# Head outputs turned in an earlier step of the head loop, and half of the first output-projection products put among the samples' small products

## The reference, cut to what matters

```python
for l in range(DEPTH):                                  # 2 layers
    hn = rmsnorm(xp, norm_mix[l])
    q_nope, q_rope, c_kv, k_r, qb, kb, vb, g = project_in(hn, pos_p, w_in[l], ...)
    a_out = mla_prompt(q_nope, q_rope, c_kv, k_r, w_ukv[l])                 # 6 heads x 64
    b_out = combine_dilations([dilated_prompt(qb, kb, vb, w, d) ...])       # 6 heads x 64
    c_out = conv_module(g_ext, conv_w[l], conv_b[l], conv_ln_g[l], ...)     # 256 channels, layer norm, silu
    xp = xp + jnp.concatenate([a_out, b_out, c_out], axis=-1) @ w_out[l]    # (256 x 1024) @ (1024 x 1024)
    hf = rmsnorm(xp, norm_ffn[l])
    xp = xp + peer_blocked(hf, peer_wq[l], peer_subkeys[l], peer_u[l], peer_v[l])
    ...                                                 # the 8 sample tokens likewise, against cache and windows
```

## Time and profile before

| | |
|---|---|
| median of 3 runs | 2055.27 us (2052.07 to 2057.17) |
| profiled execution: its time / its span | 2057.03 us / 2055.2 us |
| mean granted TensorE clock in it | 0.993 of full speed |
| PE busy | 2035.2 us (99%) |
| PEld busy | 1806.4 us (88%) |
| DVE busy | 1551.5 us (75%) |
| ACT busy | 1291.0 us (63%) |
| POOL busy | 121.5 us (6%) |

### The profile page before, as it was taken

How to read it: one execution, slowest core, us unless ns; L and a number is a source line. 1 busy time by engine, 2 the same in 40 slices (tenths; PEclk the granted TensorE clock), 3 DMA queues, 4 the chain that set the end, 5 groups by cost and what they waited for, 6 DMA issues and landing times.

```text
span 2055.2 us, 40772 instructions
## 1 busy us (share of the span) xinstructions
PE 2035.2 (99%) x15562; PEld 1806.4 (88%) x15562; DVE 1551.5 (75%) x3543; ACT 1291.0 (63%) x2567; POOL 121.5 (6%) x140
## 2 busy tenths in 40 slices
PE   9999999999999999999999999999999999999998
PEld 7777899999999888788887779999999998887887
DVE  6855789868899776676678466989588996766766
ACT  5456345658888666565564554565688876655654
POOL 2200010000000010100022000000000001101000
PEclk9999999999999999999999999999999999999999
DMA  9354357776666898898764633677767668988886
GB/s 329 142 172 154 135 170 255 244 250 222 218 208 219 290 313 289 295 322 281 250 229 143 204 133 124 214 255 251 245 215 219 216 214 307 314 284 295 268 270 219
DMA packets 137376, 481.76 MB, mean 234 GB/s; under 512 B 25666, under 2 KB 42082, under 8 KB 130768
## 3 DMA queue, kind: packets, MB, share of 16 engines
q1 hardware_dynamic: 124640, 438.45, 63.8%
q0 software_dynamic: 10496, 40.42, 5.6%
q10 hardware_dynamic: 2048, 0.30, 0.1%
HBM read 475.83 MB, written 104.21 MB: 282 GB/s over the span
## 4 chain that ended last, share of the span: by engine, by line
PE 97%; DVE 1%; ACT 1%; issue 0%; DMA 0%; ACTq 0%; DVEq 0%
PE ps L1235 36%; PE ps L1282 33%; PE ps L849 4%; PE ps L937 3%; PE ps L1247 3%; PE ps L1198 2%; PE ps L945 2%; PE ps L1206 2%; PE ps L1202 2%; PE ps L1162 1%; PE ps L893 1%; PE ps L1036 1%; PE ps L1221 1%; PE ps L902 1%; ACT region L1463 1%; PE ps L996 1%
## 5 line engine op out<-in xcount | busy, mean ns | idle before, releaser
L2231 DVE TENSOR_TENSOR parts<-region,parts 128x1024 fp32r<-128x1024 f32 x512 | 625.7, 1222 | 300.5 <-ACT parts L1559 298.6
L1235 PE MATMUL ps<-tokens_hi,parts 128*128 128x256 f32 x4096 | 760.5, 284 | 0.0
L1559 ACT CAST parts<-region 128x1024 fp32r<-128x1024 f32 x512 | 538.8, 1052 | 270.9 <-PE ps L1282 198.3
L1282 PE MATMUL ps<-parts,parts_hw 128*128 128x512 f32 x3024 | 688.7, 389 | 0.0
L1282 PEld LDWEIGHTS ps<-parts,parts_hw 128*128 128x128 f32 x3024 | 566.7, 188 | 124.1 <-DVE parts_hw L2281 6.9
L1235 PEld LDWEIGHTS ps<-tokens_hi,parts 128*128 128x128 f32 x4096 | 636.6, 188 | 1.0 <-issue 0.5
L1235 PE MATMUL ps<-parts_hw,parts 128*128 128x256 f32 x2048 | 573.7, 280 | 0.0
L1235 PEld LDWEIGHTS ps<-parts_hw,parts 128*128 128x128 f32 x2048 | 386.5, 189 | 0.0
L1605 ACT ACTIVATE big<-ps 128x256 f32<-128x256 f32 (+31 forms) x252 | 131.7, 523 | 146.9 <-PE ps L1235 146.9
L1593 ACT CAST parts_hw<-big 128x256 fp32r<-128x256 f32 x256 | 171.0, 668 | 0.7 <-DVE big L2292 0.7
L1586 ACT ACTIVATE region<-region 128x128 f16<-128x128 f16 x512 | 169.2, 436 | 0.0
(11 more groups left out here) (329 smaller groups left out, 2228.8 us busy)
## 6 DMA issues: line engine op xcount, KB each, us to landing
region<-in_peer_uT SPq DMA_DIRECT2D x256, 512.0 KB, 4.0
region<-in_peer_v SPq DMA_DIRECT2D x256, 512.0 KB, 4.8
out<-in_state_win_k SPq DMA_DIRECT2D x112, 384.0 KB, 5.0
out<-in_state_win_v SPq DMA_DIRECT2D x112, 384.0 KB, 5.0
big<-in_window_keysT SPq DMA_DIRECT2D x16, 576.0 KB, 5.6
big<-in_state_win_v SPq DMA_DIRECT2D x48, 192.0 KB, 4.0
region<-in_w_out SPq DMA_DIRECT2D x4, 2048.0 KB, 7.8
big<-in_peer_wq SPq DMA_DIRECT2D x4, 2048.0 KB, 11.2
```

The costliest lines, as they stand in the source:

```text
L1235: mm = pe.matmul(ps[:, j % ZB, 0:SEQ], a, hp[b][:, c, :], start=(c == 0 and n == 0), stop=(c == KD - 1 and n == 2))
L1282: mm = pe.matmul(ps[:, 2 * half + t, :], w_t[a][:, 128 * t:128 * t + 128], v_t[b][:, 512 * half:512 * half + 512], start=(j == 0 and n == ...
L1559: act.copy(hi_t[n % HIGHS], rows_t[n % ROWS]).then_inc(high[l], 1)
L2231: dve.tensor_tensor(lo_t[n % ROWS], rows_t[n % ROWS], hi_t[n % HIGHS], ALU.subtract).then_inc(low[l], 1)
```

## The change

Four of the six `mT` jobs move from behind the loop into step 11, ahead of `ow`; the fifth goes to step 12; the sixth stays behind the loop. The products of `out_high(0, 0)` for k = 0 to 3 move into step 12, ahead of `owT`, and those of `out_high(0, 1)` for k = 0 to 3 into step 13, ahead of `olT` (eight products each). ACT's eight weight casts and four of its casts of head outputs move into step 11, ahead of its reads of `ow`; DVE's low parts move likewise. The banks from the last `PT` to the output projection are dealt out over six banks, so that the two of the projection's first sums stay free. One block of weights (k = 5) gets another place in memory.

```diff
+EARLY = 4
...
         if s == WINDOW_MIX:
+            jobs += [(("mT", g), "V") for g in range(EARLY)]
             jobs += [(("ow", 0), "A"), (("ow", 1), "A")]
         if s == WINDOW_MIX + 1:
             jobs += [(("owT",), "V"), (("wT",), "V")]
+            jobs += [(("mT", EARLY), "V")]
...
-    jobs += [(("mT", g), "V") for g in range(2 * HP)]
+    jobs += [(("mT", EARLY + 1), "V")]
...
+    if NUM["PT", 2 * NH - 1] <= n < NUM["xo", 0, 0]:
+        return BESIDE_OUT[(n - NUM["PT", 2 * NH - 1]) % 6]
...
                     if s == WINDOW_MIX:
+                        wait_moved(pe, "O", 2 * EARLY - 1)
+                        for g in range(EARLY):
+                            turn_heads(g)
                         mix_window(0)
                         mix_window(1)
                     if s == WINDOW_MIX + 1:
+                        wait_moved(pe, "mT", EARLY - 1)
+                        out_high(0, 0, 0, EARLY)
                         wait_moved(pe, "ow", 1)
...
+                        wait_moved(pe, "O", 2 * EARLY + 1)
+                        turn_heads(EARLY)
                     if s == WINDOW_MIX + 2:
+                        out_high(0, 1, 0, EARLY)
                         pe.wait_ge(wsel_ready, 1)
...
                 wait_moved(pe, "O", 2 * NH - 1)
-                for g in range(2 * HP):
-                    turn("mT", g, parts=[...])
+                turn_heads(EARLY + 1)
...
                 for t in range(2):
-                    out_high(0, t)
+                    out_high(0, t, EARLY, KD)
...
                     if s == WINDOW_MIX:
+                        for g in range(EARLY):
+                            high_heads(g)
+                        act.wait_ge(product[now[0]], NUM["S", 2 * NH - 1] + 1)
+                        out_weights_high(0)
                         for n, dst in enumerate((owS, owS2)):
...
+                    if s == WINDOW_MIX + 1:
+                        high_heads(EARLY)
...
-                out_weights_high(0)
-                for g in range(2 * HP):
-                    ...
+                high_heads(EARLY + 1)
```

More of the change, by code:

```diff
@@ L155, with bank_of @@
 LATE = {("z", 0, 0): 0, ("z", 0, 1): 1, ("z", 0, 2): 2, ("z", 1, 2): 3, ("s", 0, 3): 4, ("s", 1, 3): 5, ("slot", 0): 6, ("pT",): 7, ("pr",): 6, ("slot", 1): 7, ("hB", 0): 4, ("hB", 1): 5, ("gy",): 6}
-BANK = [LATE.get(name, (n if n < NUM["mT", 0] else n + 6) % 8) for n, (name, _) in enumerate(JOBS)]
+OUT_BANK = [(NUM["xo", 0, t] + 6) % 8 for t in range(2)]
+BESIDE_OUT = [b for b in range(8) if b not in OUT_BANK]
+def bank_of(n, name):
+    if name in LATE:
+        return LATE[name]
+    if NUM["PT", 2 * NH - 1] <= n < NUM["xo", 0, 0]:
+        return BESIDE_OUT[(n - NUM["PT", 2 * NH - 1]) % 6]
+    return (n if n < NUM["os",] else n + 6) % 8
+BANK = [bank_of(n, name) for n, (name, _) in enumerate(JOBS)]
 PRIOR = [max([m for m in range(n) if BANK[m] == BANK[n]], default=None) for n in range(len(JOBS))]
@@ L364, in out_high_part @@
                 return rounded[24576][:, 512 * k:512 * k + 512]
-            return rounded[4096][:, 4096 + 512 * k:4608 + 512 * k] if k < 6 else rounded[11392][:, 512 * k - 3072:512 * k - 2560]
+            return rounded[4096][:, 4096 + 512 * k:4608 + 512 * k] if k < 5 else rounded[11392][:, 512 * k - 2560:512 * k - 2048]
         def out_low_part(c, k):
@@ L1085, in mix_window, with turn_heads, out_high @@
                               skip_group_check=True).then_inc(product[now[0]], 1)
+                def turn_heads(g):
+                    turn("mT", g, parts=[(oAB[:, t, 128 * g:128 * g + 128], 128, 128, 128 * t) for t in range(2)])
+                def out_high(c, t, k0, k1):
+                    o = begin("xo", c, t) if k0 == 0 else bank("xo", c, t)
+                    for k in range(k0, k1):
+                        pe.wait_ge(wo_high, KD * c + k + 1)
+                        if c == 0 and k == 2 * HP:
+                            wait_moved(pe, "ycT", 1)
+                        for i, part in enumerate((hiT, mix_lo)):
+                            pe.matmul(o[:, 0:512], part[:, k, 128 * t:128 * t + 128], out_high_part(c, k), start=(k == 0 and i == 0), stop=False,
+                                      skip_group_check=True)
                 for s in range(2 * NH + 2):
@@ L1139, in _ @@
                 wait_moved(pe, "O", 2 * NH - 1)
-                for g in range(2 * HP):
-                    turn("mT", g, parts=[(oAB[:, t, 128 * g:128 * g + 128], 128, 128, 128 * t) for t in range(2)])
+                turn_heads(EARLY + 1)
                 wait_moved(pe, "olT")
@@ L1154, in _ @@
                 wait_moved(pe, "os")
[L1155 to L1163, removed]
                 def out_low(c, t):
@@ L1454, in _, with out_weights_high, high_heads @@
                     act.copy(va[:, t, :], o[:, 0:384]).then_inc(moved_a[now[0]], 1)
+                def out_weights_high(c):
+                    act.wait_ge(w_ld[now[0]][(5 + c) % 2], 16 * ((5 + c) // 2))
+                    for k in range(KD):
+                        act.copy(out_high_part(c, k), wview(5 + c)[:, k, :]).then_inc(wo_high, 1)
+                def high_heads(g):
+                    o = arrive(act, "mT", g)
+                    act.copy(hiT[:, g, 0:SEQ], o[:, 0:SEQ]).then_inc(mix_high, 1)
                 for s in range(2 * NH + 2):
@@ L1514, in _ @@
                             act.copy(yt[0:m, t, :], o[0:m, 0:CC]).then_inc(moved_a[now[0]], 1)
+                    if s == WINDOW_MIX + 1:
+                        high_heads(EARLY)
                     if s == CONV_STEP[3]:
                         roots(5, slice(9, 12))
[L1517 to L1520, removed]
-                out_weights_high(0)
-                for g in range(2 * HP):
-                    o = arrive(act, "mT", g)
-                    act.copy(hiT[:, g, 0:SEQ], o[:, 0:SEQ]).then_inc(mix_high, 1)
+                high_heads(EARLY + 1)
                 for c in range(2):
@@ L1992, in conv_out, with low_heads @@
                         wait_moved(dve, "ycT", c)
+                def low_heads(g):
+                    o = read("mT", g)
+                    dve.wait_ge(mix_high, g + 1)
+                    dve.tensor_tensor(mix_lo[:, g, 0:SEQ], o[:, 0:SEQ], hiT[:, g, 0:SEQ], ALU.subtract).then_inc(moved_v[now[0]], 1)
                 for s in range(2 * NH + 2):
@@ L2023, in _ @@
                         part_logits()
+                    if s == WINDOW_MIX:
+                        for g in range(EARLY):
+                            low_heads(g)
                     if s == WINDOW_MIX + 1:
@@ L2026, in _ @@
                         part_weights()
+                        low_heads(EARLY)
                     if s == WINDOW_MIX + 2:
@@ L2035, in _ @@
                         conv_norm()
[L2036 to L2039, removed]
+                low_heads(EARLY + 1)
                 o = read("os")
```

2 lines of the change are left out of this document (1 added, 1 removed).

## The result

The changed kernel takes 2058.80 us (median of 9 runs, 2057.43 to 2062.33), the kernel before 2052.15 beside it (9 runs, 2051.61 to 2057.17): a ratio of 1.0029, with a 95% interval of 1.0020 to 1.0037, or 6.0 us more. That is no difference by the bound of 0.3% set ahead, though only just, and all of the interval lies on the slow side. The forecast was 2058.0, made as 2.8 us on a median of 2055.27: the time is met, the difference is twice as large.

What follows compares the result with a forecast made beforehand. PE carries 97% of the chain, then hands over to DVE in the output projection. That hand-over 1.4 us later in each of two layers gives +2.8 us on the median of 2055.27: 2058.0 us, range 2052 to 2063.

Steps and rivals of the forecast that it cites:

- The mechanism: Output projection: PE waits for `conv_out` with 12 high products queued behind, the first nine at 1.2 GHz; 1.4 us later per layer.
- The hand-over to DVE: Layer 0's output projection: DVE carries the chain from 197.88 us, so its earlier or later start shifts all behind.
- Three signs of being right: PE idle 2 to 4 us for `conv_out`; `conv_out` ending some 2.6 us later; second `add_out` 0.1 to 2.0 later.
- the cost of a layer: Up to DVE's hand-over: 1.4 us later per layer, bounds 0.1 if the clock holds, 2.0 if all 12 run at 1.2.
- In the kernel before this hides: Convolution's chain before the change: PE needs it only with its 13th product, near 189.3 us, after `conv_out` ends at 188.24.
- the path to the last `mT` product: Steps 11 to 13 on PE: last `mT` product near 184.7 us against 182.1, 2.6 us later.
- What stands behind the start of the batch: From `conv_out`'s end at 190.8: 12 high products to 195.3, then 16 low products and the pipeline, 3.9 us, to 199.2.
- all products behind the new wait begin at 1.2 GHz: Products behind PE's wait for `conv_out`: the skill's rule that each burst after a wait begins cold; gives the 1.4 us.
- The clock holds: Rival: wide products among small ones keep 2.4 GHz, back at once after the wait; +0.1 us a layer, 2055.5 us; chance 0.29.
- No wait: Rival: PE's wait for the convolution doesn't bind, low clock's price returns; 4.3 us earlier a layer, 2046.7 us; chance 0.05.
- Early fall: Rival: clock falls near 182 us, in the second early batch; 4.5 taken, 2064.3 us; chance 0.14.

Runs made afterwards that it cites:

- convolution early: Changed kernel with the convolution's norm, transposes, sigmoid, `conv_out` and last head pair ahead of the second eight early products, `os` behind the high products: 2047.02 us, ratio to before 0.9971.
- the version with the convolution's products last: Changed kernel with the first tile's products for k = 6 and 7 behind the second tile's k = 4 and 5: 2055.60 us, ratio to before 1.0013.
- its longer chain: Kernel before with `conv_out`'s first DVE instruction of the first 128 tokens run three times instead of once: 2055.92 us, ratio to before 1.0019.
- the heads alone early: Changed kernel with the sixteen early output-projection products put back behind the convolution's transposes: 2054.13 us, ratio to before 1.0007.
- the convolution early with the products late: Version with the convolution's part moved ahead, but its sixteen early products put back behind the convolution's transposes: 2053.22 us, ratio to before 0.9998.

## Why the prediction was right, and where its sizes were off

The stage by execution, us after the exponential of head 11 (PE's start behind its wait for the convolution, the wait in brackets, and DVE's second `add_out`):

| execution | layer 0 | layer 1 |
|---|---|---|
| before, first | no wait, 30.89 | no wait, 30.89 |
| before, second | 21.23 (1.69), 29.88 | 21.01 (1.47), 29.70 |
| before, third | no wait, 30.93 | 20.19 (1.74), 28.84 |
| after, first | 24.50 (1.80), 33.00 | 24.40 (2.07), 33.32 |
| after, second | 24.39 (3.48), 32.55 | 24.39 (1.80), 33.12 |
| convolution early | no wait, 27.40 | no wait, 27.39 |

The means are 30.19 before and 33.00 after: 2.8 us in a layer, 5.6 in both, of the 6.0 measured (4.1 to 7.6 by the interval).

**Right.** The mechanism is the one that was forecast. The hand-over to DVE does set the layer: from layer 0's second `add_out` to layer 1's exponential all executions without a fall of the clock in between agree within 0.5 us (986.6 to 987.04). PE waits for the last instruction of `conv_out` in both layers, 1.8 and 2.1 us, with 12 high products behind it, 1.2 GHz in the wait, and the first of these products 0.43 apart, eight and a half and ten and a half of the twelve (nine forecast). The clock stood at 1.00 from 175 to 181.9. ACT's copy of head 10's probabilities held PE for 0.62 us ahead of the fourth early pair (0.6 forecast), and the last page did not wait for `ow` 0: no idle time stands ahead of its row at 172.60. The weights landed in time as in the earlier trace rows (median 7.8 us after their issue), and ACT's casts of the query weights, 1.5 us later in the stage than before (188.12), were done long before DVE came to them (197.76). Three signs of being right were met in kind but not in size: the waits of 1.80 and 2.07 us lie at or under the lower end of 2 to 4, `conv_out` ended 3.1 and 2.6 us later against some 2.6, and the second `add_out` came 2.1 and 2.4 us later against 0.1 to 2.0.

**The term that was mis-sized: the cost of a layer, forecast 1.4 us, measured 2.8 (2.1 and 2.4 between the two first traces).** The sum had a layer end 32.2 us after the exponential (199.2 less 166.99), against 30.89 before. The means are 33.00 and 30.19. So some 0.7 us is missing on either side.

The first is "In the kernel before this hides". The earlier trace rows bear that out, but for that execution alone, whose clock was low for 10 us in both layers. In three layers of six PE waits for the convolution in the kernel before as well. The stage I started from was one of the long ones: 30.89 against 30.19 in the mean.

The second is the path to the last `mT` product and on to the last batch. By the prediction's times `conv_out` ends at 190.8, 23.8 us after the exponential; the batch began 24.39 to 24.50 after it in all four layers. In the first trace each batch of eight took 2.0 to 2.1 us up to the next product, where 1.87 was put; the last head cast began 0.56 us behind the start of its two transposes (181.70), where 0.24 was put; and `ow` began 1.77 us after the exponential, where 1.6 was put. What stands behind the start of the batch was sized well: 8.4 us forecast, 8.2 to 8.9 measured.

Where the clock is at 2.4 GHz in both kernels, the new path costs more still. DVE starts `conv_out` 20.59 us after the exponential (after, second execution, layer 0) against 16.40 (before, third, layer 1), 4.2 us later; between the two first traces it was 3.1 and 2.6, because the path of before had run partly at 1.2. Of the 4.2 us 1.7 lie ahead of `ow`, which starts 1.76 us after the exponential and not 0.06: the eight transposes and PE's wait of 0.62. The other 2.5 are, by my estimate, the sixteen products, 16 x 0.234 = 3.7, less 1.2 for the transposes and casts that left the end of the chain. So the layer at its best stands thus: 4.2 later, less 1.9 (eight of the 20 products no longer behind the wait, 8 x 0.234), plus 1.4 for the first seven of the twelve at 1.2 GHz: 3.7, and 32.55 - 28.84 is 3.7.

**The Trainium skill's rule** ("TensorE: Matmul & The Clock Gate", section "HAM oscillation — how this bites in real kernels"), by which a burst behind a wait begins cold, is a rule for waits beyond a certain length; the prediction left that condition out. The clock did fall inside the wait of 3.48 us in the changed kernel (1.00 ahead of it, 0.50 behind it) and inside that of 2.54 us in the version with the convolution's products last. The waits in the section's own example are longer than 2.54 us. Behind the waits of 1.47, 1.69 and 1.74 us in the kernel before the products ran at 1.00, so "all products behind the new wait begin at 1.2 GHz" does not follow from a wait alone. For the waits of 1.80 and 2.07 the trace says nothing on it, since the clock had fallen before.

**The rivals.** "The clock holds" was wrong behind the wait, and right up to it in one layer of four. "No wait" was wrong here, and is what the version with the convolution early makes of it: I gave it 2046.7, and that version takes 2047.02; that the two times agree is luck, since the gain was forecast at 8.6 us and is 5.2. "Early fall" did not come. The fall at 181.9 looks like the one it names (before 182), but the exponential comes 3.07 us earlier in this execution than in the one from which the prediction counts. By the prediction's times the fall is near 185, behind its last transposes at 184.7.

**The baseline.** I put the profiled execution at 1.8 us above the median of three runs and took that as an offset. It was more than that: by the medians of 9 to 30 runs beside the later kernels, before takes 2052.1 to 2052.2, 3.1 us less. That the predicted time came within 1 us of the measured one is luck: two errors of some 3 us with opposite signs.

What stays open is why the low clock lasts 3 to 4 us in some layers and executions of one kernel and 10 in others; no experiment here set it.

## What to carry to other kernels

Work that is moved ahead to fill an engine's thin stretch also stands ahead of whatever that stretch feeds: follow the longest chain that leaves it through other engines (here a cast, a table load, a sigmoid, 8 vector instructions), and move the start of that chain first. A wait that one trace doesn't show may be hidden only because the engine was slow in that execution; look at the stage in each layer and in a second execution before calling it covered. Times of two executions are compared from an event that both share, not from the start of the span. And where a wait can't be removed, count what stands behind it, once at each of the two clocks.

## What the runs showed of the hardware

TensorE's clock fell and returned at different places in executions of one and the same kernel: in layer 1 of the kernel before it was low for 10.3, 3.4 and 0 us in three executions. Its place in the stage goes with the order of PE's work. Of the twelve profiled layers without the early wide products (the kernel before three times, its longer chain, the heads alone early, the convolution early with the products late) eleven have a fall, 10.6 to 15.1 us after the exponential of head 11. Of the twelve with them ten have one, 17.8 to 24.2 us after it; the version with the convolution early has none.

Two further falls, of 1.7 us of lost time each and 24 us apart, are in some executions and not in others (near 86 and 110 us, or, in the second execution of the changed kernel, near 1106 and 1130). By estimate these (3.4 us) and the stage's own variation (28.84 to 30.93 us in a layer) can make up most of the 2050 to 2058 us over which runs of the kernel before spread; only the profiled runs have a trace, so this is not shown. The version whose stage has neither a wait nor a long run of small products spreads less in most of its runs (seven of eight from 2046.3 to 2047.9).
